# A streaming-encoder block on eight cores: first-pass gates block by block with weight slots of their own, and both first FFN units in slices of K

## The chip, the cores and the metric

The kernel runs on all 8 NeuronCores of one Trainium2 chip; cores 0 to 3 are one die, 4 to 7 the other. The cores share nothing while they run: each does one eighth of the sequence positions, and loads all weights itself. The metric is the device time of the slowest core in microseconds. Everything below is read from one profiled execution, on its slowest core (core 7), unless another is named.

## The reference, cut to what matters

```python
def reference(x, c, ...):          # x (2, 8192, 1024); D_FF 2816, 8 heads of 64
    mod = silu(c) @ w_ada + b_ada  # shift, scale, gate for each of three sub-layers
    h = modulate(rms_norm(x, g_ffn1), sh1, sc1)
    a, b = split(h @ w_ffn1_in)
    x = x + 0.5 * gt1 * ((silu(a) * b) @ w_ffn1_out)

    h = modulate(rms_norm(x, g_mix), sh2, sc2)
    q, k, v, u, ga, gb = split(h @ w_in)
    ya = chunk_band_attention(q, k, v, ...) @ w_attn_out  # own chunk of 64 and 8 before it
    yb = multiscale_pool(u, w_pool_group, pool_scale) @ w_pool_out
    x = x + gt2 * ((sigmoid(ga) * ya + sigmoid(gb) * yb) @ w_o)

    h = modulate(rms_norm(x, g_ffn2), sh3, sc3)
    ...                                                   # a second FFN like the first
    return x
```

## The kernel before, in words

A core owns 2048 positions, held transposed (features on partitions) as four blocks of 512 columns, blocks 1 to 4, and recomputes one more block ahead of them, block 0 (the halo), because attention and pooling look back. Three stages follow each other: the first FFN over blocks 0 to 4, the mixer, and the second FFN over blocks 1 to 4. Nearly all TensorE work is matmuls of 128x128 weights against 512 columns in bf16, eight of them (over K) for one output tile.

**The order is planned, not written.** The code emits operations through `S.op` with an engine, a cost, what it reads and writes, and a priority (`S.prio`). `Sched.schedule` then simulates the five engines and picks, for each, the ready operation with the lowest priority number that can start first. The resulting list of each engine is fixed in the program; every engine then works through its list strictly in order. In the mixer the priorities come from the table `RAMPS`: for instance "a0" is the first attention pass, "k3" and "q4" are key and query projections, "g0" the gates of the first pass. The planner also simulates the DMA queues (`drain`), with a latency and a share for GpSimd's and SyncE's queue. A change of a number in the table, or of a rule in the planner, moves work on every engine.

**The start.** SyncE loads the halo and block 1; GpSimd loads the first eight chunks of `w_ada` (conversion from f32 to bf16 in the DMA) with the first FFN weight tile `W1ST` between chunks 5 and 6. Each `w_ada` chunk feeds 16 one-column matmuls (`ada_mm`, L573), whose result is a piece of shift or scale. Chunks 4 to 7 bring the scales: after each, `norm_late` (DVE L675, ACT L671) makes two of the eight 128-row slices of the normalised input of blocks 0 and 1. `norm_late(1, ...)` stands behind the loop over the chunks in the code. A `unit` is one hidden tile of the FFN for one block: eight matmuls for the a half, eight for the b half, then SiLU on ACT and a product on DVE. The very first unit (block 0) is issued slice by slice as the input slices appear (L729, 16 matmuls in all); every other unit is issued whole (L738). Block 2's x is loaded by SyncE once the last `w_ada` chunk (`ADA[7]`) is in.

**The mixer** works in two passes over the owned blocks, 1 and 2 and then 3 and 4. Queries, keys and values are projected (`kq_unit` L922 with a one-matmul sum of squares L929, `v_tile` L905); `att_pair` handles two heads and 256 queries: three groups of score matmuls (L968), exponentials on ACT, multiplication with a bias table on DVE, 20 matmuls with V (L1004), a normalisation and a transposition (L1017). `u_stage` is the pooling branch (L1048, L1062, L1087). `gates` computes, for each of eight output tiles n and each of the pass's two blocks mb, two 8-matmul gate tiles (L1116), two 4-matmul branch tiles (L1129), and their gated sum into `MRG`. `oproj` (L1148) multiplies `MRG` with `w_o`. PSUM has eight banks, and the planner places each tile.

**Weight places.** A load takes the next slot of a ring of 4 KB slots per partition. Ring "m" has six slots and serves queries, keys, values, gates and `w_o`. The gates of a pass use three tiles per pair of output tiles, twelve loads in all, each used for both blocks. Ring "u" is one slot, `o_wx`, in the x buffer of block 4, which is spilled to memory in the meantime. A load whose slot is still read waits on GpSimd's queue, and everything behind it in that queue waits too.

## Time and profile before

| | us |
|---|---|
| three runs | 1826.21, 1827.65, 1531.79 (median 1826.21) |
| the profiled execution, its own time | 1537.52 |
| its span, first to last instruction, core 7 | 1535.9 |
| spans of the eight cores | 1522.5 to 1535.9 |
| busy: TensorE | 1482.4 |
| busy: VectorE | 853.5 |
| busy: ScalarE | 471.4 |

The span is the time between the first and the last instruction of a core; the execution's own time is 1.6 us more. "Busy" of TensorE counts matmuls; weight loads overlap them. The granted clock is 1.00 at 2.4 GHz and 0.50 at 1.2 GHz. The three runs lie at two levels; the profiled execution is at the lower one. The first FFN runs until about 640 us, the mixer until about 1070, the second FFN from there to the end.

### The profile page before, as it was taken

To read this page: it belongs to the slowest core of one execution; us is meant where nothing else is said; L and a number is where in the kernel's file an instruction comes from. 1 tells how busy PE (TensorE), PEld (TensorE's weight loads), DVE (VectorE), ACT (ScalarE), POOL (GpSimd) and SP (SyncE) were. 2 spreads that over 40 slices of the span, in tenths; PEclk is the share of its full clock that TensorE was granted. 3 is DMA by queue.
4 is the path that set the end of the run, shared out by engine and by line. 5 is a ranking of instruction groups with operands and counts; after the bars stand their busy time and mean duration, and the time that the engine had idled before them with its cause. 6 is when DMAs were issued, how large, how long until landed. Compare 5 with 4: busy or idle time off the path is not lost.

```text
span 1535.9 us, 22662 instructions; the slowest of 8 cores (1522.5 to 1535.9 us)
## 1 busy us (share of the span) xinstructions
PE 1482.4 (97%) x7952; PEld 695.3 (45%) x7952; DVE 853.5 (56%) x1336; ACT 471.4 (31%) x658; POOL 104.7 (7%) x146
## 2 busy tenths in 40 slices
PE   2899999999999999999999999999999999999998
PEld 1344444444444444455554544444444444444443
DVE  2365557374484745677865668456352616262644
ACT  3460110101101046787775551345401010101010
POOL 1100000000000012200000000302000000000000
PEclk8799999999999999999999999999999999999999
DMA  9946443524415110420053355348033221211022
GB/s 207 246 84 103 87 133 77 152 61 123 135 39 143 22 44 1 142 52 15 2 124 56 58 101 104 55 83 135 10 56 56 42 41 22 42 28 28 1 110 110
DMA packets 28478, 120.21 MB, mean 78 GB/s; under 512 B 3280, under 2 KB 3536, under 8 KB 26320
## 3 DMA queue, kind: packets, MB, share of 16 engines
q0 software_dynamic: 17856, 63.09, 24.6%
q1 hardware_dynamic: 10512, 55.67, 10.4%
q8 instruction: 67, 1.10, 0.3%
q14 instruction: 43, 0.35, 0.1%
HBM read 169.24 MB, written 12.58 MB: 118 GB/s over the span
## 4 chain that ended last, share of the span: by engine, by line
PE 92%; DMA 3%; DVE 2%; ACT 1%; issue 1%; POOL 0%; DVEq 0%; ACTq 0%; POOLq 0%; SPq 0%
PE ps L738 44%; PE ps L771 22%; PE ps L1116 7%; PE ps L922 4%; PE ps L1129 4%; PE ps L1148 3%; PE ps L905 2%; DMA arena<-w_ada 2%; PE ps L1062 2%; PE ps L968 1%; PE ps L1004 1%; PE ps L630 1%; ACT arena L514 1%; DVE arena L520 1%; DMA arena<-w_adat 1%
## 5 line engine op out<-in xcount | busy, mean ns | idle before, releaser
L738 PE MATMUL ps<-arena 128*128 128x512 bf16 x3152 | 691.3, 381 | 2.8 <-DVE arena L520 2.7
L514 ACT ACTIVATE arena<-ps 128x512 bf16<-128x512 f32 (+3 forms) x426 | 269.7, 652 | 936.2 <-PE ps L738 770.1
L738 PEld LDWEIGHTS ps<-arena 128*128 128x128 bf16 x3152 | 309.3, 98 | 380.4 <-issue 19.1
L526 DVE SCALAR_TENSOR_TENSOR arena<-ps,arena 128x512 f32<-128x512 f32 (+1 forms) x500 | 359.8, 747 | 76.2 <-ACT arena L514 19.7
L771 PE MATMUL ps<-arena 128*128 128x512 bf16 x1584 | 348.2, 381 | 1.9 <-DVE arena L520 1.1
L520 DVE TENSOR_TENSOR arena<-arena,ps 128x512 bf16<-128x512 bf16 x198 | 135.1, 686 | 367.2 <-PE ps L738 357.1
L771 PEld LDWEIGHTS ps<-arena 128*128 128x128 bf16 x1584 | 155.5, 98 | 191.3 <-issue 11.6
L520 DVE TENSOR_TENSOR arena<-arena 128x1024 bf16<-128x1024 bf16 (+10 forms) x229 | 174.7, 779 | 44.5 <-ACT arena L514 38.1
L1116 PE MATMUL ps<-arena 128*128 128x512 bf16 x512 | 116.2, 379 | 0.6 <-DMA arena<-w_gate 0.6
L514 ACT ACTIVATE arena<-arena 128x512 f32<-128x512 f32 (+2 forms) x87 | 90.5, 1054 | 42.8 <-DVE arena L526 26.5
L604 DVE SCALAR_TENSOR_TENSOR arena<-arena 128x1024 f32<-128x1024 f32 x48 | 58.7, 1224 | 64.2 <-DMA arena<-w_adat 63.7
L1116 PEld LDWEIGHTS ps<-arena 128*128 128x128 bf16 x512 | 48.9, 98 | 59.2 <-issue 1.4
L526 DVE SCALAR_TENSOR_TENSOR arena<-arena,ps 128x512 f32<-128x512 f32 x64 | 43.8, 686 | 50.9 <-PE ps L1129 45.9
L922 PE MATMUL ps<-arena 128*128 128x512 bf16 x288 | 67.5, 382 | 0.2 <-ACT arena L515 0.2
L1129 PE MATMUL ps<-arena 128*128 128x512 bf16 x256 | 60.6, 379 | 0.4 <-DVE arena L526 0.4
L1148 PE MATMUL ps<-arena 128*128 128x512 bf16 x256 | 59.2, 387 | 0.5 <-ACT arena L514 0.5
L515 ACT ACTIVATE arena<-arena 128x512 bf16<-128x512 f32 x63 | 48.2, 805 | 18.0 <-DVE arena L520 18.0
L520 POOL TENSOR_TENSOR arena<-arena 128x1024 bf16<-128x1024 bf16 x18 | 38.5, 2144 | 114.0 <-ACT arena L514 114.0
L922 PEld LDWEIGHTS ps<-arena 128*128 128x128 bf16 x288 | 27.5, 98 | 32.0 <-issue 3.5
L1148 PEld LDWEIGHTS ps<-arena 128*128 128x128 bf16 x256 | 25.2, 99 | 31.4 <-issue 5.7
L515 ACT ACTIVATE arena<-ps,arena 128x512 f32<-128x512 f32 x50 | 34.2, 684 | 14.2 <-PE ps L630 6.9
L905 PE MATMUL ps<-arena 128*128 128x256 bf16 x320 | 37.8, 273 | 0.3 <-ACT arena L515 0.3
(67 smaller groups left out, 489.7 us busy)
## 6 DMA issues: line engine op xcount, KB each, us to landing
arena<-w_adat SPq DMA_DIRECT2D x48, 512.0 KB, 4.1
arena<-w_gate POOLq DMA_DIRECT2D x24, 512.0 KB, 7.3
arena<-w1i POOLq DMA_DIRECT2D x22, 512.0 KB, 8.2
arena<-w3i POOLq DMA_DIRECT2D x22, 512.0 KB, 5.2
arena<-x SPq DMA_DIRECT2D x5, 2048.0 KB, 14.8
outT<-arena SPq DMA_DIRECT2D x7, 1024.0 KB, 3.9
arena<-w_ada POOLq DMA_DIRECT2D x12, 512.0 KB, 24.3
arena<-w1o POOLq DMA_DIRECT2D x10, 512.0 KB, 8.1
```

The source lines that it names most:

```text
L514: return e.activation(out=o, in_=i, func=func, scale=scale)
L515: return e.activation(out=o, in_=i, func=func, bias=bias, scale=scale)
L520: return e.tensor_tensor(out=out() if callable(out) else out, in0=in0() if callable(in0) else in0, in1=in1() if callable(in1) else in1, op=op)
L526: return e.scalar_tensor_tensor(out=out, in0=in0() if callable(in0) else in0, scalar=scalar, in1=in1() if callable(in1) else in1, op0=op0, ...
L604: S.op("dve", lambda e: e.scalar_tensor_tensor(out=wt, in0=wt, scalar=1.0, in1=CCB, op0=ALU.mult, op1=ALU.mult, accum_out=MOD[:, j:j + 1]) ...
L738: ins = e.matmul(pst(t), lhsT=w[:, kt, :], rhs=hk(b, kt), start=(kt == 0), stop=(kt == 7))
L771: ins = e.matmul(pst(t), lhsT=wos[jl // 2][:, c0:c0 + 128], rhs=hd[jl], start=(jl == 0), stop=(jl == nk - 1))
L905: ins = e.matmul(pst(tl, hf * 256, hf * 256 + 256), lhsT=H[:, b, kt, t * 128:(t + 1) * 128], rhs=w[:, kt, :], start=(kt == 0), stop=(kt == 7))
L922: ins = e.matmul(pst(raw), lhsT=w[:, kt, f * 128:(f + 1) * 128], rhs=hk(b, kt), start=(kt == 0), stop=(kt == 7))
L1116: ins = e.matmul(pst(tg), lhsT=wg[:, kt, fs], rhs=hk(b, kt), start=(kt == 0), stop=(kt == 7))
L1129: ins = e.matmul(pst(ty), lhsT=w[:, hp, fs], rhs=src[:, hp, ms], start=(hp == 0), stop=(hp == 3))
L1148: ins = e.matmul(pst(to), lhsT=w[:, kt, (n % 2) * 128:(n % 2 + 1) * 128], rhs=MRG[:, kt, ms], start=(kt == 0), stop=(kt == 7))
```

## The change

1. `RAMPS` is a new table of numbers, with an entry "g0a" for the gates of block 1 alone. The planner's DMA model is changed: a landing latency `DLAT` of 2.6 instead of 2.0, and a transfer doesn't move before this latency has passed.
2. `gates(0, ...)` is split. The gates of block 1 are emitted right behind the pooling stage, with a ring "e" of three slots: two in the second half of `MRG`, and `o_wx`. The gates of block 2 stand where both stood, with ring "m". All twelve weight tiles are loaded once for each block, so the first pass has 24 gate loads. `MRG` is laid out by block, so that block 1's half is whole while the other half holds weights.
3. The first unit of block 0 and the first unit of block 1 are issued together in pieces of two K slices (`pieces`, L732): for each pair of slices, block 0's a and b, then block 1's a and b.
4. `norm_late(1, ...)` moves into the loop over chunks; block 2's x is loaded behind `ADA[6]`; in block 2's first normalisation ACT does four slices of eight instead of three.

```diff
+    DLAT = 2.6
...
-                            work[k].pop(0)[1].fin = now + 2.0
+                        work[k].pop(0)[1].fin = now + self.DLAT
...
-    MRG = view(o_mrg, BF16, (8, 1024))
+    MRG = view(o_mrg, BF16, (2, 8, TB))
...
+             "e": [o_mrg + 8192, o_mrg + 12288, o_wx]}
...
-                if kt in ((1, 4, 7) if sub == 0 else (0, 1, 3, 4, 6, 7)):
+                if kt in ((1, 3, 5, 7) if sub == 0 and b == 2 else (1, 4, 7) if sub == 0 else (0, 1, 3, 4, 6, 7)):
...
-    norm_late(1, range(8))
+            norm_late(1, (2 * k, 2 * k + 1))
...
+        def pieces(wt, bs):
+            wv = [wt[:, 1024 * i:1024 * i + 1024].rearrange("p (k n) -> p k n", k=8) for i in range(2)]
+            tl = {b: (Tile(), Tile()) for b in bs}
+            for k in range(4):
+                for b in bs:
+                    for t, w in zip(tl[b], wv):
+                        def mm(e, t=t, w=w, b=b, k=k):
+                            ins = None
+                            for kt in (2 * k, 2 * k + 1):
+                                ins = e.matmul(pst(t), lhsT=w[:, kt, :], rhs=hk(b, kt), start=(kt == 0), stop=(kt == 7))
+                            return ins
+                        S.op("pe", mm, reads=[wt, H[:, b, 2 * k:2 * k + 2, :]] + ([t] if k else []), writes=[t],
+                             cost=mmc(2, 512), also=[tl[b][1]] if t is tl[b][0] and k == 0 else (), stream="ab")
+            return tl
+
+        def unit(jl, b, wt, last=False, pre=None):
...
-            split = first and ucount[0] == 0
+            split = pre is not None
+            if split:
+                ta, tb = pre
...
-                    for b, after in ((2, ADA[7][1]), (3, wl[2][1]), (4, wl[3][1])):
+                    for b, after in ((2, ADA[6][1]), (3, wl[2][1]), (4, wl[3][1])):
...
+                            pcs = pieces(wts[0], (0, 1))
                             for jl in range(nk):
-                                unit(jl, 0, wts[jl])
-                                unit(jl, 1, wts[jl])
+                                unit(jl, 0, wts[jl], pre=pcs[0] if jl == 0 else None)
+                                unit(jl, 1, wts[jl], pre=pcs[1] if jl == 0 else None)
...
-    def gates(pas, pr):
+    def gates(pas, pr, mbs=(0, 1), ring="m"):
...
-            wga_ = load("m", gate_d[3 * c])[0]
-            wgb_ = load("m", gate_d[3 * c + 1])[0]
-            wap = load("m", gate_d[3 * c + 2])[0]
+            wga_ = load(ring, gate_d[3 * c])[0]
+            wgb_ = load(ring, gate_d[3 * c + 1])[0]
+            wap = load(ring, gate_d[3 * c + 2])[0]
...
-                for mb in range(2):
+                for mb in mbs:
...
     u_stage(0, ramp(*R["u0"], 8))
+    gates(0, ramp(*R["g0a"], 8), (0,), "e")
...
-    gates(0, ramp(*R["g0"], 16))
+    gates(0, ramp(*R["g0"], 8), (1,))
```

Of the table, the line with "a0" before and now, and the new entry "g0a":

```diff
-         "a0": (5.02, 11.48), "u0": (10.18, 20.6), "k3": (13.33, 13.57), "k4": (11.61, 26.2),
...
+RAMPS = {"g0a": (9.83, 12.94), "nb": (-2.29, 8.29), "f2": (-9.48, -7.81), "f3": (3.97, 5.97),
...
+         "v0b": (16.07, 20.14), "a0": (2.73, 9.57), "u0": (11.7, 21.52), "k3": (15.22, 22.54),
```

**Where instructions move.** Names are line numbers of each version; equal neighbours are counted together.

TensorE at the start, before: the sliced unit of block 0 (L729) between the one-column matmuls of the `w_ada` chunks (L573), then whole units (L738).

```order
L573 MATMUL ps<-arena 128x1 x48
L729 MATMUL ps<-arena 128x512 x8
L573 MATMUL ps<-arena 128x1 x16
L729 MATMUL ps<-arena 128x512 x4
L573 MATMUL ps<-arena 128x1 x16
L729 MATMUL ps<-arena 128x512 x4
L738 MATMUL ps<-arena 128x512 x56
```

And now (L576 one-column matmuls, L732 sliced, L751 whole):

```order
L576 MATMUL ps<-arena 128x1 x64
L732 MATMUL ps<-arena 128x512 x16
L576 MATMUL ps<-arena 128x1 x16
L732 MATMUL ps<-arena 128x512 x6
L576 MATMUL ps<-arena 128x1 x16
L732 MATMUL ps<-arena 128x512 x10
L751 MATMUL ps<-arena 128x512 x40
```

Block 1's first 16 matmuls have moved from behind the last chunk to between the chunks: 16 stand ahead of chunk 6's matmuls instead of 8, 6 ahead of chunk 7's instead of 4, and 10 behind it instead of 4.

GpSimd's queue from the last fold of block 4 in the first FFN (TENSOR_TENSOR) to the first pass's gate weights, before:

```order
L520 TENSOR_TENSOR arena<-arena 128x1024
L868 DMA arena<-w_pg 128x512
L870 DMA arena<-ident 128x128
L498 DMA arena<-w_kqvu 128x2048 x2
L498 DMA arena<-w_gate 128x2048 x12
L498 DMA arena<-w_o 128x2048 x4
```

And now:

```order
L523 TENSOR_TENSOR arena<-arena 128x1024 x8
L501 DMA arena<-w_gate 128x2048 x2
L523 TENSOR_TENSOR arena<-arena 128x1024
L501 DMA arena<-w_kqvu 128x2048
L523 TENSOR_TENSOR arena<-arena 128x1024
L882 DMA arena<-w_pg 128x512
L501 DMA arena<-w_kqvu 128x2048
L884 DMA arena<-ident 128x128
L501 DMA arena<-w_kqvu 128x2048
L501 DMA arena<-w_gate 128x2048 x22
L501 DMA arena<-w_o 128x2048 x4
```

Two gate loads have moved ahead of the last folds, and 22 (with two ahead of them, 24) stand where 12 stood. Ten of the 22 are for ring "e", twelve for ring "m", mixed.

TensorE in the first attention pass, before: the end of the longest stretch that holds only attention (L968 scores, L1004 products with V, L1017 transpositions; the eight matmuls of 16 columns, L1048, are the pooling branch's halo), up to a key or query projection (L922). Its first three rows, L1017, L968 and L1004, stand just ahead.

```order
L968 MATMUL ps<-arena 128x128 x4
L968 MATMUL ps<-arena 128x256 x4
L1048 MATMUL ps<-arena 128x16 x8
L968 MATMUL ps<-arena 128x256 x4
L1017 MATMUL ps<-arena 128x128 x2
L968 MATMUL ps<-arena 128x128 x4
L968 MATMUL ps<-arena 128x256 x4
L1004 MATMUL ps<-arena 128x65 x20
L968 MATMUL ps<-arena 128x256 x4
L968 MATMUL ps<-arena 128x128 x4
L1017 MATMUL ps<-arena 128x128 x2
L922 MATMUL ps<-arena 128x512 x8
```

And now the longest such stretch (L982 scores, L1018 products, L1031 transpositions, L936 projection); one row of two score groups stands just ahead:

```order
L1018 MATMUL ps<-arena 128x65 x20
L982 MATMUL ps<-arena 128x128 x4
L982 MATMUL ps<-arena 128x256 x4
L1031 MATMUL ps<-arena 128x128 x2
L982 MATMUL ps<-arena 128x256 x4
L982 MATMUL ps<-arena 128x128 x4
L1018 MATMUL ps<-arena 128x65 x20
L982 MATMUL ps<-arena 128x256 x8
L1031 MATMUL ps<-arena 128x128 x2
L1018 MATMUL ps<-arena 128x65 x20
L982 MATMUL ps<-arena 128x128 x4
L936 MATMUL ps<-arena 128x512 x8
```

The stretch has moved to another place of the pass and holds three products with V instead of two.

## Rows read from the trace of the kernel before

**Rows 1.** The page, its first line and part 1: the span, and TensorE's busy time.

```profile
span 1535.9 us, 22662 instructions; the slowest of 8 cores (1522.5 to 1535.9 us)
...
PE 1482.4 (97%) x7952; PEld 695.3 (45%) x7952; DVE 853.5 (56%) x1336; ACT 471.4 (31%) x658; POOL 104.7 (7%) x146
```

**Rows 2.** Windows of 20 us: PE, PEld, DVE, ACT, POOL busy; clock, DMA share, GB/s.

```profile
40.00:60.00 20.00, 15.75 (x75) 6.48 (x76) 6.01 (x15) 5.90 (x9) 0.76 (x1) 0.59 1.03 224
120.00:140.00 20.00, 19.15 (x138) 9.22 (x137) 8.55 (x16) 2.61 (x4) 2.64 (x5) 0.91 0.71 130
```

**Rows 3.** Timeline of TensorE, 40 to 84 us: start, duration, line, count, idle before.

```profile
41.33 3.57 PE L729 MATMUL ps<-arena 128*128 128x512 bf16 x8 [3.23 <-DVE arena L675]
44.69 0.61 PE L573 MATMUL ps<-arena 128*128 128x1 bf16 x16
46.89 1.86 PE L729 MATMUL ps<-arena 128*128 128x512 bf16 x4 [1.59 <-ACT arena L671]
...
50.49 1.86 PE L729 MATMUL ps<-arena 128*128 128x512 bf16 x4 [1.33 <-DVE arena L675]
52.15 14.33 PE L738 MATMUL ps<-arena 128*128 128x512 bf16 x56
...
81.45 2.27 PE L630 MATMUL ps<-arena 128*128 128x512 bf16 x8
```

**Rows 4.** Windows of 4 us; the number after POOL is the granted clock.

```profile
52.00:56.00 4.00, 4.00 (x11) 1.33 (x10) 0.69 (x1) 2.01 (x3) 0.00 (x0) 0.50 0.99 270
56.00:60.00 4.00, 4.00 (x19) 1.79 (x18) 0.69 (x1) 0.79 (x2) 0.00 (x0) 0.96 0.99 282
```

**Rows 5.** Timeline of SyncE's queue, 40 to 84 us.

```profile
47.21 17.71 SPq L802 DMA_DIRECT2D arena<-x  x3
```

**Rows 6.** DMA queues, 36 to 44 us: queue, packets, MB, share of 16 engines.

```profile
q0 software_dynamic: 358, 1.32, 100.3%
```

**Rows 7.** DMA queues, 54 to 62 us: same columns.

```profile
q1 hardware_dynamic: 112, 1.57, 56.3%
q0 software_dynamic: 151, 0.55, 45.3%
```

**Rows 8.** Timeline of ScalarE, 75 to 90 us: block 2's last normalised slice.

```profile
81.92 0.80 ACT L515 ACTIVATE arena<-arena 128x512 bf16<-128x512 f32 x1
```

**Rows 9.** Windows of the mixer stage, same columns as rows 2.

```profile
640.00:980.00 340.00, 330.32 (x2538) 175.63 (x2537) 237.92 (x440) 204.15 (x302) 30.52 (x39) 1.00 0.33 68
680.00:760.00 80.00, 74.57 (x820) 45.49 (x818) 64.84 (x142) 62.37 (x89) 0.53 (x1) 1.00 0.05 8
900.00:920.00 20.00, 18.80 (x129) 8.96 (x128) 13.05 (x24) 9.71 (x14) 1.58 (x3) 1.00 0.63 116
```

**Rows 10.** Who TensorE waited for, 640 to 980 us: total us, times, longest.

```profile
PE ps L968 <- ACT arena L514: 3.3, 9, 0.6
```

**Rows 11.** Tile view of w_gate: issue to landing, all 24 loads.

```profile
DMA to landing us min/median/max: 5.1/7.3/9.0
```

**Rows 12.** Timeline of TensorE, 905 to 950 us: the one wait for a gate weight.

```profile
945.64 1.89 PE L1116 MATMUL ps<-arena 128*128 128x512 bf16 x8 [0.64 <-DMA arena<-w_gate]
```

**Rows 13.** Timeline of GpSimd, 938 to 948 us: the load behind that wait.

```profile
939.25 0.53 POOL L498 DMA_DIRECT2D arena<-w_gate  x1 [13.21 <-PE ps L1017]
```

**Rows 14.** Timeline of TensorE, 745 to 755 us: attention without other work.

```profile
748.29 0.39 PE L968 MATMUL ps<-arena 64*128 64x256 bf16 x4
748.62 0.78 PE L1004 MATMUL ps<-arena 128*128 128x65 bf16 x20
...
751.43 0.39 PE L968 MATMUL ps<-arena 64*128 64x256 bf16 x4 [0.54 <-ACT arena L514]
...
753.76 0.27 PE L1017 MATMUL ps<-arena 128*128 128x128 bf16 x2 [0.64 <-DVE arena L520]
```

**Rows 15.** Groups by line and form, 700 to 780 us: exponentials of scores, 512-column reads.

```profile
L514 ACT ACTIVATE arena<-ps 128x1024 bf16<-128x1024 f32 x26 | 25.7, 1023 | 4.2 <-PE ps L968 2.9 <-DVE arena L520 0.8 <-DVE arena L526 0.4
...
L514 ACT ACTIVATE arena<-ps 128x512 bf16<-128x512 f32 x28 | 16.4, 595 | 12.4 <-PE ps L922 9.6 <-DVE arena L1010 1.3 <-PE ps L968 1.3
```

More of the change, by code:

```diff
@@ L249, in drain @@
             while (work["pool"] or work["sp"]) and (until is None or now < until):
-                both = work["pool"] and work["sp"]
+                live = [k for k in work if work[k] and work[k][0][2] <= now + 1e-9]
+                both = len(live) == 2
                 share = {"pool": 1.0 - self.SPSHARE, "sp": self.SPSHARE} if both else {"pool": 1.0, "sp": 1.0}
-                step = min(work[k][0][0] / share[k] for k in work if work[k])
+                step = min([work[k][0][0] / share[k] for k in live] +
+                           [work[k][0][2] - now for k in work if work[k] and k not in live])
                 if until is not None:
@@ L255, in drain @@
                 now += step
[L256 to L260 removed]
+                for k in live:
+                    work[k][0][0] -= step * share[k]
+                    if work[k][0][0] <= 1e-9:
+                        work[k].pop(0)[1].fin = now + self.DLAT
             if until is not None:
@@ L1142, in oproj, with mmo @@
             to = Tile()
[L1144 removed]
+            def mmo(e, to=to, n=n, mb=mb):
                 ins = None
```

28 lines of the change are left out of this document (7 added, 21 removed), and 8 rows, old and new, of the table RAMPS.

## Prediction

> **What bounds the kernel now.** Look first at the page: TensorE is busy 1482.4 us of a span of 1535.9 [rows 1], so all its idle time together is 53.5 us. The change adds and removes no matmul (7952 before), so it can gain only idle time and time at the lower clock. Two per cent, which is about what a measurement of this kernel can tell from no change, are 30.7 us.
>
> Then the windows, to see where the idle time lies. The first sliced unit starts at 41.33 us [rows 3]; ahead of it stand loads whose order the change keeps. From 640 to 980 us, the mixer, TensorE is busy 330.32 of 340 us: 9.7 us idle. 5.4 of these lie between 680 and 760 us, in the first attention pass, and 1.2 between 900 and 920 [rows 9]. The FFN stages have almost none, and their order is nearly the same. So the change works on two places: the stretch from 41 to 84 us, and 9.7 us of the mixer.
>
> Last, the rows inside the two places. At the start the granted clock is 0.59 between 40 and 60 us [rows 2], 0.50 until 56 and 0.96 behind it [rows 4]: matmuls cost about double until then. In the mixer the waits are short and many: TensorE's scores (L968) waited for exponentials on ACT, 3.3 us in nine waits [rows 10].
>
> **The start, step by step.** Eight sliced matmuls take 3.57 us [rows 3], 0.446 each at 1.2 GHz; from 56 to 60 us, nearly all at 2.4 GHz, 4 us hold 19, 0.21 each [rows 4]. Before: 16 matmuls of block 0 are issued between the chunks, with idle gaps of 1.59 and 1.33 us for the slices, and block 1's 16 start at 52.15. Their end: 3.85 us at the low clock until 56.0 hold 8.6 matmuls, 7.4 more at 0.21 take 1.6, so 57.6 us.
>
> After, in the order shown: 16 matmuls from 41.33, at 0.446, end at 48.5. Chunk 6's one-column matmuls (0.61) were at 44.69 and now come behind them, a delay of 3.8 us for that chunk, and scale, slices and the rest are late with it: end 49.1. The gap of 1.59 stays, since the next six need that chunk: 50.7. Six matmuls: 53.4. Chunk 7: 54.0. Two matmuls hide 0.9 of the gap of 1.33: 55.3. The last eight: if the clock rises at 56 as before, 1.6 slow and 6.4 fast ones take 2.0, end 57.3. That is 0.3 us better than before. If the clock stays low to the end, 8 take 3.6: 58.9, so 1.3 worse. If the clock rises inside the first block of 16, say for its last four, then these and the 16 behind them cost 0.236 less each, 4.7 us in all: end about 54.2 at best, 3.4 better. I take 1.5 better, between the neutral case and the good one, because the change closes most pauses between 41 and 53 us, and the row before shows the clock coming back 4 us after TensorE had begun to issue without pause at 52.15. Ends: 1.3 worse, 3.4 better.
>
> The row shows what TensorE did: pauses of 1.33 to 3.23 us among short blocks, and a clock at 1.2 GHz until 56 [rows 3, 4]. The Trainium skill, "TensorE: Matmul & The Clock Gate", section "HAM oscillation — how this bites in real kernels", advises to run the K slices of a tile together ahead of a wait so that the array stays at full clock. By that rule 16 matmuls in a row ahead of chunk 6 would bring the good end and not the value taken; it has its place among the rivals.
>
> Is the gain kept? Block 2 must be normalised when blocks 0 and 1 are done. Its last slice was ready at 81.92 + 0.80 = 82.7 us, and TensorE began block 2 behind the eight sums, at 81.45 + 2.27 = 83.7 [rows 3, 8]: cover of 1.0 us. The change pays for this. Block 2's x was issued at 47.21 [rows 5] and is now issued behind chunk 6, whose matmuls ran at 44.69, so 2.5 us earlier or more, and one of VectorE's slices moves to ACT. So cover of 1.0 + 2.5 = 3.5 against a gain of at most 3.4. In return chunk 7 has a rival for bandwidth: alone GpSimd's queue moved 1.32 MB in 8 us, beside an x block 0.55 [rows 6, 7]. If the last 0.15 MB of chunk 7 go at 0.069 instead of 0.165 MB/us, it lands 1.3 us later, ahead of its place in TensorE's order (53.4, where it was 46.89 + 1.86 = 48.7): no cost. The next weight tiles come later too, by some 3 us, and are needed at 55 to 57; I leave 0 to 1 us for it and take 0. The move of `norm_late(1)` costs and brings nothing: VectorE's order at the start reads as before, since the planner had mixed the two already.
>
> **The mixer, step by step.** *Gate loads.* 12 more loads of 0.5 MB (f32 in memory) ride on queues whose DMA share is 0.05 between 680 and 760 us and 0.33 over the stage [rows 9]: bandwidth is no cost. What can cost is time to turn a slot round: the three slots of ring "e" hold just one group of weights, so each load waits for the last reader and must land before the group after it. Load issue to landing took 5.1 to 9.0 us, median 7.3 [rows 11]. In the new order I counted the TensorE work between release and next use for the ten loads concerned, at 1.7 us per eight matmuls and the attention times below: 9.0, 10.5, 10.5, 13.4, 9.0, 12, 14, 10, 10.3 and 12 us. Allowing 0.5 us until GpSimd issues, the median load has 1.2 us to spare in the tightest cases, the slowest is 0.5 late. The one measured case: a load issued at 939.25 with its use ready at 945.0 cost 0.64 us at 945.64 [rows 12, 13], with 6.4 us for it. So 0 for most; I take 0.5, ends 0 and 5 (ten times 0.5). That wait at 945.64 itself has 11 us of cover in the new order: gain 0.6. GpSimd's queue runs in order: behind the two early gate loads stand the last folds of block 4's sums; the slots are free once a bias table is exponentiated on ACT, and the square which the fold needs stands behind that on ACT anyway: 0.
>
> *Attention.* In the longest stretch without other work, TensorE spent 748.29 to 753.76 = 5.5 us, of which 0.54 + 0.64 = 1.2 idle [rows 14]. The new stretch has 6 large and 3 small score groups, 3 products with V (one is 0.78) and 2 transpositions: about 5.2 us of work when the older one's 4.3 is scaled up by one product and one score group less a transposition. ACT needs for its three pairs 3 x (2 x 1.023 + 0.595) = 7.9 us [rows 15]. So its idle time is between 1.2 (as measured) and 7.9 - 5.2 = 2.7 us; the old stretch is gone, -1.2. Net 0 to +1.5; take +0.5. For the remaining 4.2 us between 680 and 760 the ingredients are the same (k, q, v and pooling as filler), so what falls and what rises is open: -3 to +3, take -1. The gates of block 1, which ask most of TensorE and least of ACT, now fill the end of this pass and the begin of the next; but there (760 to 900) little idle time is left to take. *900 to 920 us.* 1.2 us idle there, where the last gate and first `w_o` matmuls met; their new places are apart: -0.6, ends 0 and -1.2.
>
> Sum of the mixer: 0.5 - 0.6 + 0.5 - 1 - 0.6 = -1.2. The layout of `MRG` changes no operand's contiguous 512 columns: 0.
>
> **The forecast.** -1.5 - 1.2 = -2.7 us on the profiled execution's own 1537.5, so 1534.8, or 0.2%. The runs shown lie at 1531.8 and at 1826 to 1828; the profile belongs to the lower, from which it is 5.7 off, and its median of 1826.21 says nothing on this execution. I give the time on the lower level, from its run: 1531.8 - 2.7 = 1529. At the upper level the same share would leave it unchanged within 4 us.
>
> **The rivals.** *The clock comes back inside the slices* (chance 0.15), as under the rule above: 3.4 at the start and 1.2 in the mixer, 1527. For it speaks the block of 16 matmuls without a pause, against it that TensorE pauses again behind it for 1.6 us. *The idle time of the mixer really closes* (0.20). For it: gates are large blocks of TensorE work with light ACT and DVE work, ready early. Most of 9.7 us goes, say 8, with 3 at the start: 1521. Against it: the attention pass already had filler at most places, and waited for ACT all the same.
>
> *Slower: ring "e" is turned too late* (0.12). Place: `gates` of block 1, four groups. If loads land 9 us or more behind their issue (two rings' loads are mixed in one queue, and six are at times issued together), each of three turns costs 2 to 3 us on TensorE, +8 us, with no gain in the start: 1539. It decides from a landing of 8.6 us in the tightest cases; against it stands the median of 7.3.
>
> *Slower: attention loses its filler* (0.15). The new stretch shows the upper bound and others join it: +2.7 + 3, start +1: 1537. By the Trainium skill, "TensorE: Matmul & The Clock Gate", section "A second HAM failure mode: psum-queue depth-cycling", frequent short pauses between groups of matmuls make the clock fall and rise again. As a mechanism here: more pauses in the first pass, and the clock at 0.5 for a while; one drop, as that between 120 and 140 us where 64 one-column matmuls ran and the mean clock was 0.91 [rows 2], costs 1.8 us, three 5.4: 1537 with the rest (0.03 of the 0.15). The trace disagrees with that rule so far: 5.4 us of pauses in 80, and clock 1.00 [rows 9].
>
> *It does not do what it says* (0.08): the slices give nothing and the orders are worth the same: 1531 to 1532.
>
> **How the numbers follow.** Forecast 0.30, the rivals as above. The bounds of the terms go from -3.4 - 8 to +1.3 + 8; the range 1519 to 1542 holds all but about one in six. A gain of 30.7 us would need more than all idle time outside the first 41 us; a loss of that size needs a queue held up for tens of us, which no bound shows. So faster 0.02, within 2% 0.95, slower 0.03.
>
> **What would show it.** In the new profile: the last of the 32 sliced matmuls ends between 54.2 and 58.9 us, with the granted clock of 44 to 56 us above 0.5 if the good end holds; TensorE doesn't wait before block 2's first unit; idle time of TensorE from 640 to 980 between 6 and 12 us; waits of L1130 or L1143 for w_gate below 1 us in total; the stretch of pure attention with 1 to 3 us idle. Wrong it would be if a wait for w_gate of over 2 us appears, if block 2's normalisation is waited for, or if idle time shows up in the FFN stages.

## The result and the profile after

The changed kernel takes 1535.6 us (median of nine runs, 1534.3 to 1538.6), the kernel before 1531.3 beside it. The ratio is 1.0029 with a 95% interval of 1.0020 to 1.0039: some 4.4 us slower, where I had forecast 2.7 us faster. Ratios, here and below, leave out executions in which one die ran at a lower clock than the other.

The profiled execution's page begins as follows [rows 1]. TensorE's busy time fell by 6 us at the same 7952 matmuls, since more of them met the full clock (mean of the first 84 us on core 7: 0.96 against 0.79). That is this core in these two executions and not the change: the median of the eight cores is 0.91 in both kernels. The span hardly moved, so idle time grew.

```profile
span 1535.2 us, 22697 instructions; the slowest of 8 cores (1526.1 to 1535.2 us)
...
PE 1476.4 (96%) x7952; PEld 693.6 (45%) x7952; DVE 853.2 (56%) x1335; ACT 482.0 (31%) x667; POOL 112.1 (7%) x158
```

The start on core 7, TensorE's timeline [rows 3]. The first block of 16 ran as counted, then 6, 2 and 8; the last sliced matmul ends at 54.48 + 3.57 = 58.05. Block 2's norm is waited for 0.33 us (at 80.90).

```profile
41.83 6.56 PE L732 MATMUL ps<-arena 128*128 128x512 bf16 x16 [3.26 <-DMA arena<-w1i]
...
50.48 2.00 PE L732 MATMUL ps<-arena 128*128 128x512 bf16 x6 [1.71 <-DVE arena L678]
...
52.75 1.01 PE L732 MATMUL ps<-arena 128*128 128x512 bf16 x2
54.48 3.57 PE L732 MATMUL ps<-arena 128*128 128x512 bf16 x8 [0.71 <-ACT arena L674]
...
80.90 3.40 PE L751 MATMUL ps<-arena 128*128 128x512 bf16 x15 [0.33 <-ACT arena L518]
```

The mixer's windows on core 7, columns as in [rows 9]:

```profile
640.00:980.00 340.00, 322.96 (x2483) 170.03 (x2482) 231.62 (x435) 217.02 (x312) 30.64 (x45) 0.99 0.49 84
640.00:660.00 20.00, 15.50 (x99) 9.47 (x98) 13.16 (x17) 14.31 (x22) 1.63 (x3) 0.97 1.00 213
660.00:680.00 20.00, 19.51 (x101) 9.37 (x99) 8.03 (x17) 14.44 (x22) 0.00 (x0) 0.94 0.11 28
680.00:700.00 20.00, 16.32 (x149) 8.89 (x149) 13.56 (x29) 15.69 (x24) 0.53 (x1) 0.91 0.21 27
680.00:760.00 80.00, 70.04 (x720) 42.46 (x721) 59.88 (x128) 54.72 (x80) 0.53 (x1) 0.98 0.06 8
900.00:920.00 20.00, 19.38 (x171) 9.76 (x170) 15.58 (x32) 13.63 (x20) 1.58 (x3) 1.00 0.83 165
```

Idle time of the stage went from 9.7 to 17.0 us, and from 660 to 700 us the granted clock is 0.94 and 0.91 where before had 1.00. The window of 640 to 660 us stands out: 4.5 us idle, and the DMA engines full. Before, the same window reads:

```profile
640.00:660.00 20.00, 19.75 (x118) 11.49 (x117) 15.74 (x18) 15.87 (x24) 5.79 (x5) 0.95 0.61 174
```

The wait behind it is found in three steps. TensorE's timeline of the changed kernel has one long wait, for ScalarE:

```profile
653.85 1.89 PE L1130 MATMUL ps<-arena 128*128 128x512 bf16 x8
658.49 3.29 PE L936 MATMUL ps<-arena 128*128 128x512 bf16 x8 [2.75 <-ACT arena L518]
```

ScalarE's timeline at that time: it had no work that it was allowed to begin, since the next in its list was the exponential of the bias table's second quarter (`tab`: four loads by SyncE, two exponentials of 128x640 for each), and that was still on its way.

```profile
651.85 0.63 ACT L517 ACTIVATE arena<-arena 128x512 f32<-128x512 f32 x1
656.30 1.36 ACT L517 ACTIVATE arena<-arena 128x640 bf16<-128x640 f32 x2 [3.82 <-DMA arena<-tab]
```

The tile view of `tab`, changed kernel first and then before: the slowest of four loads took 14.0 us from issue to landing, where it was 5.7.

```profile
DMA to landing us min/median/max: 4.6/5.8/14.0
```

```profile
DMA to landing us min/median/max: 3.7/3.8/5.7
```

What moves beside it: SyncE spills blocks 3 and 4 (2 MB each, issued at 625.92 and some 8 us later) and GpSimd has the first two gate loads of ring "e" in flight from 630.56 on. Cores 0, 6 and 7 show 3.7, 4.5 and 4.5 us of idle time from 640 to 660; they have the longest spans (1532.9, 1534.9, 1535.2). Core 2 with 0.6 us there has the shortest, 1526.1, and a clock of 1.00 from 640 to 760 us.

Who TensorE waited for from 640 to 740 us on core 7, first the changed kernel, then before:

```profile
PE ps L982 <- ACT arena L517: 3.2, 7, 0.8
PE ps L936 <- ACT arena L518: 2.8, 1, 2.8
PE ps L943 <- ACT arena L517: 1.4, 4, 0.6
PE ps L1031 <- DVE arena L523: 0.9, 2, 0.5
PE ps L919 <- ACT arena L518: 1.1, 1, 1.1
PE ps L1062 <- DVE arena L535: 1.1, 1, 1.1
PE ps L1018 <- DVE arena L1083: 0.9, 1, 0.9
PE ps L1101 <- ACT arena L518: 0.7, 1, 0.7
PE ps L936 <- DVE arena L535: 0.5, 1, 0.5
PE ps L1076 <- DVE arena L535: 0.5, 1, 0.5
```

```profile
PE ps L968 <- ACT arena L514: 2.3, 6, 0.6
PE ps L1004 <- ACT arena L514: 0.7, 1, 0.7
PE ps L929 <- ACT arena L514: 0.7, 3, 0.2
PE ps L1017 <- DVE arena L520: 0.3, 1, 0.3
```

Attention (L982, L1018, L1031; before L968, L1004, L1017) waited 3.3 us before and 5.5 now. Projections (L919, L936, L943; before L922, L929) and pooling (L1062, L1076, L1101) waited 0.9 us before and 8.7 now, shorter rows of 0.2 to 0.4 us included in all four sums. So most of the loss isn't in the attention, but in the work meant to fill it; 2.8 us of it are the one wait behind the late table. For `w_gate` seven cores never wait, the eighth 0.3 us.

### The profile page after: what moved, and what is told of

Read it like the earlier page. It is cut to its first block, busy times and chain, and to the rows that moved or that the text cites. A ratio compares the mean times of both kernels' runs of the same rounds, so it can differ in the third digit from the quotient of the medians.

```text
span 1535.2 us, 22697 instructions; the slowest of 8 cores (1526.1 to 1535.2 us)
## 1 busy us (share of the span) xinstructions
PE 1476.4 (96%) x7952; PEld 693.6 (45%) x7952; DVE 853.2 (56%) x1335; ACT 482.0 (31%) x667; POOL 112.1 (7%) x158
## 4 chain that ended last, share of the span: by engine, by line
PE 91%; DMA 3%; DVE 2%; ACT 2%; issue 1%; POOL 0%; DVEq 0%; ACTq 0%; SPq 0%; POOLq 0%
PE ps L751 43%; PE ps L784 21%; PE ps L1130 7%; PE ps L936 4%; PE ps L1162 4%; PE ps L1143 4%; DMA arena<-w1i 2%; PE ps L1076 2%; PE ps L919 2%; PE ps L982 1%; PE ps L1018 1%; DMA arena<-tab 1%; DVE arena L523 1%; ACT arena L517 1%; PE ps L732 1%
## 5 line engine op out<-in xcount | busy, mean ns | idle before, releaser
L751 PE MATMUL ps<-arena 128*128 128x512 bf16 x3136 | 681.5, 379 | 0.3 <-ACT arena L518 0.3
L751 PEld LDWEIGHTS ps<-arena 128*128 128x128 bf16 x3136 | 306.9, 98 | 370.9 <-issue 1.5
L784 PEld LDWEIGHTS ps<-arena 128*128 128x128 bf16 x1584 | 154.8, 98 | 188.9 <-issue 4.5
L523 DVE TENSOR_TENSOR arena<-arena 128x1024 bf16<-128x1024 bf16 (+11 forms) x229 | 174.7, 782 | 33.9 <-ACT arena L517 28.2
L1130 PEld LDWEIGHTS ps<-arena 128*128 128x128 bf16 x512 | 49.3, 98 | 59.0 <-issue 1.0
L936 PE MATMUL ps<-arena 128*128 128x512 bf16 x288 | 68.8, 385 | 3.6 <-ACT arena L518 3.1
L936 PEld LDWEIGHTS ps<-arena 128*128 128x128 bf16 x288 | 27.3, 98 | 36.0 <-issue 7.5
L919 PE MATMUL ps<-arena 128*128 128x256 bf16 x320 | 37.5, 273 | 1.8 <-ACT arena L518 1.1
```

What stands on the lines that cost most here:

```text
L523: return e.tensor_tensor(out=out() if callable(out) else out, in0=in0() if callable(in0) else in0, in1=in1() if callable(in1) else in1, op=op)
L751: ins = e.matmul(pst(t), lhsT=w[:, kt, :], rhs=hk(b, kt), start=(kt == 0), stop=(kt == 7))
L784: ins = e.matmul(pst(t), lhsT=wos[jl // 2][:, c0:c0 + 128], rhs=hd[jl], start=(jl == 0), stop=(jl == nk - 1))
L919: ins = e.matmul(pst(tl, hf * 256, hf * 256 + 256), lhsT=H[:, b, kt, t * 128:(t + 1) * 128], rhs=w[:, kt, :], start=(kt == 0), stop=(kt == 7))
L936: ins = e.matmul(pst(raw), lhsT=w[:, kt, f * 128:(f + 1) * 128], rhs=hk(b, kt), start=(kt == 0), stop=(kt == 7))
L1130: ins = e.matmul(pst(tg), lhsT=wg[:, kt, fs], rhs=hk(b, kt), start=(kt == 0), stop=(kt == 7))
```

## Experiments

Eleven kernels ran, ratios to the kernel before, five rounds each. With them the change comes apart into a front (start and first FFN) and a mixer.

### The start alone, in the old company

```diff
-    norm_late(1, range(8))
+            norm_late(1, (2 * k, 2 * k + 1))
...
-                    for b, after in ((2, ADA[7][1]), (3, wl[2][1]), (4, wl[3][1])):
+                    for b, after in ((2, ADA[6][1]), (3, wl[2][1]), (4, wl[3][1])):
...
+                            pcs = pieces(wts[0], (0, 1))
```

With `pieces` and the slices on ACT as in the change; nothing else of it.

> The kernel before, with only the start of the change: the two first units in K slices issued together, norm_late(1) in the loop, block 2's x behind ADA[6], four slices of block 2's norm on ACT. Table of numbers, planner's model, gates and rings are as before, so the mixer's order stays. My step for the start said 1.5 us faster (ends 1.3 slower, 3.4 faster). The trace after showed TensorE's idle time from 41 to 84 us about as before (3.9 against 4.4 us, median of cores). Theory A (the start is neutral, the loss is all in the mixer): 1530 to 1533, ratio to before 0.9995 to 1.0010. Rival (the start itself costs what the whole change lost): 1535 to 1536, ratio 1.0025 to 1.0035. My forecast's own step: 1529 to 1530, ratio 0.9985 to 0.9993.

Measured: 1531.6 us, 1.0007 (0.9998 to 1.0016). No gain. The timeline of core 4, whose clock was 1.00 from 48 to 64 us, shows one reason: the slices end early, and then TensorE stands at block 2's sums (and behind this wait, from 64 to 68 us, the clock is 0.57). The squares for them, on ScalarE, waited for block 2's x.

```profile
51.84 1.89 PE L729 MATMUL ps<-arena 128*128 128x512 bf16 x8 [1.59 <-ACT arena L671]
53.57 7.07 PE L748 MATMUL ps<-arena 128*128 128x512 bf16 x32
63.99 3.36 PE L630 MATMUL ps<-arena 128*128 128x512 bf16 x8 [3.36 <-ACT arena L514]
```

```profile
59.66 3.71 ACT L514 ACTIVATE arena<-arena 128x2048 bf16<-128x2048 f32 x2 [4.76 <-DMA arena<-x]
```

Cores 1, 4 and 6, with a mean clock of 0.93 to 1.00 from 41 to 60 us, wait 1.9 to 3.4 us between 60 and 84. The other five, with 0.59 to 0.78, are later and don't wait there. So the gain is eaten by this wait where the clock was high; elsewhere the low clock left none (before, the median clock of this stretch was 0.80, here 0.69). In the changed kernel the sums stand behind 40 matmuls of whole units instead of 32, and there is no such wait: the planner's longer landing time moved them.

### The changed kernel with the old start

```diff
-            norm_late(1, (2 * k, 2 * k + 1))
+    norm_late(1, range(8))
...
-                            pcs = pieces(wts[0], (0, 1))
```

The same hunks taken out of the changed kernel.

> The changed kernel with the start of before (one sliced unit, norm_late(1) behind the loop, block 2's x behind ADA[7], three slices on ACT); the new table, the planner's model and the split gates stay. Theory A (start neutral): like the changed kernel, 1535 to 1536.5, ratio to before 1.0022 to 1.0035. Rival (the start costs): 1531 to 1532. If the start gained 1.5 as forecast: 1537, ratio 1.004.

Measured: 1539.7 us, 1.0059 (1.0045 to 1.0074). Theory A (neutral start) fell, and so did both others of the expectation: in this company the start is worth 0.0030, 4.6 us, more than I had thought in any case.

### The front alone: changed front, old mixer

```diff
-                        work[k].pop(0)[1].fin = now + self.DLAT
+                        x = work[k].pop(0)[1]
+                        x.fin = now + (self.DLAT if x.idx < self.NEWTO else 2.0)
...
     ffn(w1i, w1o, 0, [0, 1, 2, 3, 4], True)
+    S.NEWTO = len(S.ops)
```

From operation `NEWTO` on the planner uses the old DMA model; `RAMPS`, gates, `MRG` and rings are as before, the start as changed.

> The start of the change and its planner's DMA model up to the end of the first FFN (a transfer lands 2.6 us after its end, and moves only 2.6 us after its issue); from the mixer on the planner counts as before, with the old table of numbers and unsplit gates, so the mixer's order is that of before. Theory E (the front part of the change is a gain, the mixer alone loses): TensorE's idle time from 140 to 560 us is 0 where it was 2.7 (median of cores), no wait of 3.4 us for block 2's sums at 64 us as in the run with the start alone, so 2 to 4 us better than before: 1526.5 to 1528.5, ratio 0.9974 to 0.9987. Rival (the front part gives back what it gains, as the run with the start alone did): 1530 to 1532, ratio 0.9995 to 1.001. My forecast's step for the start alone: 1.5 better.

Measured: 1527.5 us, 0.9980 (0.9971 to 0.9990): the front is a gain of 3.1 us, and this kernel beats both. Windows of core 7, this kernel and then before:

```profile
140.00:560.00 420.00, 420.00 (x1947) 190.38 (x1946) 251.14 (x378) 54.72 (x85) 17.96 (x28) 1.00 0.39 94
640.00:740.00 100.00, 94.92 (x872) 57.73 (x870) 76.45 (x152) 78.10 (x117) 2.36 (x4) 1.00 0.17 38
740.00:980.00 240.00, 234.46 (x1660) 116.60 (x1657) 156.30 (x284) 122.90 (x183) 23.68 (x32) 1.00 0.42 80
```

```profile
140.00:560.00 420.00, 417.21 (x1928) 188.20 (x1926) 251.64 (x379) 48.61 (x77) 16.29 (x28) 1.00 0.39 95
640.00:740.00 100.00, 95.55 (x808) 56.28 (x808) 76.55 (x144) 77.74 (x116) 6.85 (x7) 0.99 0.21 53
740.00:980.00 240.00, 234.77 (x1732) 119.35 (x1732) 161.37 (x297) 126.41 (x187) 23.68 (x32) 1.00 0.38 75
```

2.8 us idle in the first FFN are gone: four waits of up to 0.9 us of L738 for VectorE. The mixer isn't the same order (872 matmuls between 640 and 740 us instead of 808), but idles about as much as before, at a clock of 1.00.

### The planner's model in the front, with the old start

```diff
-            norm_late(1, (2 * k, 2 * k + 1))
+    norm_late(1, range(8))
...
-                            pcs = pieces(wts[0], (0, 1))
```

On the kernel above.

> As the kernel with the changed front and the old mixer, but with the start of before too: only the planner's DMA model in the first FFN is changed. Theory E: the waits of 2.7 us between 140 and 560 us go; but the changed kernel with the old start had 2.1 us of waits between 60 and 84 us for block 2's norm, where before had 0.3, so the two cancel: 1529.5 to 1531.5, ratio 0.9995 to 1.0005, and this kernel is 2 to 4 us slower than the one with the new start. Rival (the planner's model is the whole gain, and the start gives nothing in either company): 1528 to 1529, same as with the new start.

Measured: 1532.0 us, 1.0008 (0.9999 to 1.0018). A little above the 1529.5 to 1531.5 expected. So the front is two halves that only pay together:

| | old planner model | new model in the first FFN |
|---|---|---|
| old start | 1 | 1.0008 |
| new start | 1.0007 | 0.9980 |

With the old start and the new model TensorE waits 2.1 us (median of cores, 60 to 84 us) for block 2's sums and norm, which eats what the FFN gains; the new start brings block 2's x earlier (issued at 44.8 us instead of 46.7 on core 3) and takes this wait to 0.2. That is 1.9 of the 4.3 us between the two kernels. The clock from 41 to 60 us may hold the rest: its median over cores is 0.69 here and 0.91 with the new start, in one profiled execution of each.

### The gate loads held back

```diff
+            dp = [TABOP[1]] if ring == "e" and c == 0 else ()
-            wga_ = load(ring, gate_d[3 * c])[0]
+            wga_ = load(ring, gate_d[3 * c], deps=dp)[0]
```

The same for `wgb_`; `TABOP[1]` is the load of the bias table's second quarter.

> The changed kernel, but the first two gate loads of ring e wait until the bias table's second quarter (the one behind the spill of block 4 in SyncE's queue) has landed; after them the order of GpSimd's queue and a little of TensorE's moves. Theory B (the early gate loads share the DMA engines with the spills and with that table load, which landed 14.0 us after its issue on core 7 against 3.8 before, and ScalarE waited 3.82 us for it, TensorE 2.75 behind): the table lands within 6 us of its issue, ScalarE waits below 1 us for it on every core, TensorE's idle time from 640 to 660 falls from 3.1 us (median of cores) to about 1, time 1532.5 to 1534. Rival C (the spill ahead of it on SyncE's queue makes it late, not the gate loads): it still lands 10 us and more behind its issue, time as changed, 1535 to 1536. Rival D (the wait is covered or replaced: what is lost is in the new order of 660 to 740 us): the landing improves and the time stays at 1535 to 1536.

Measured: 1549.5 us, 1.0128 (1.0113 to 1.0142). No theory held. From 640 to 660 us idle time fell from 2.8 to 0.8 us (median of cores), and the slowest table load on core 7 took 8.6 us instead of 14.0. But theory B wanted 6 us and no wait of 1 us on any core: on cores 0, 2, 4 and 5 it took 10.9 to 11.7 us, and ScalarE waited 2.0 to 2.8. And the planner answered the late weights with another order, with 3.8 us idle from 660 to 680 (changed: 2.3) and 7.7 us from 860 to 980 (changed: 1.4). The time says nothing on the table.

### The exponentials moved on ScalarE

```diff
     S.schedule()
+    qa = S.q["act"]
+    for r, behind in ((2, 9), (3, 9), (6, 8), (7, 8)):
+        i = qa.index(TEXP[r])
+        qa.insert(i + behind, qa.pop(i))
```

> The changed kernel with all DMA as it is, but on ScalarE the four exponentials of the bias table's second and fourth quarter stand nine and eight places further back in the engine's list (about 6 us later), behind key projections' LN and EXP chains; nothing else moves. Theory B2 (the in-order stall of ScalarE is what the late table costs): the wait for tab falls from 3.82 us on core 7 to below 0.5, TensorE's idle 640 to 660 from 3.7, 4.5 and 4.5 us on cores 0, 6 and 7 to 1 to 2, and the slowest cores gain 2 to 3 us: 1532.5 to 1534. Rival D (another wait takes its place within 20 us, since these cores' ScalarE is as late with its work as before): 1535 to 1536, with the idle time moved to 660 to 700.

Measured: 1532.4 us, 1.0013 (1.0004 to 1.0022). Moving four instructions of 0.7 us by some 6 us gives back 0.0016 of 0.0029, 2.5 us. Core 7:

```profile
640.00:660.00 20.00, 19.39 (x123) 11.68 (x122) 12.43 (x16) 15.30 (x25) 1.63 (x3) 1.00 0.80 153
660.00:680.00 20.00, 17.48 (x95) 7.58 (x95) 10.32 (x23) 16.07 (x26) 0.24 (x1) 1.00 0.12 34
680.00:700.00 20.00, 16.81 (x171) 9.65 (x169) 16.14 (x35) 14.63 (x21) 0.29 (x1) 1.00 0.15 28
640.00:740.00 100.00, 89.21 (x783) 49.84 (x781) 68.67 (x140) 76.64 (x115) 2.15 (x4) 1.00 0.22 44
```

The table load is as late as without the edit (13.1 us from issue on core 7), and nobody waits for it. From 640 to 740 us 10.8 us of pauses remain (median of cores; changed: 12.6). So theory B2 holds: the late table had cost the wait. Whether it had also cost the clock isn't shown. In this profiled execution the granted clock is 1.00 from 640 to 700 us on all cores, but two kernels below, without the wait too, have it down to 0.91 from 680 us on. Over the timed runs the mean clock of all cores is 0.993 both here and in the changed kernel.

### The table ahead of the second spill

```diff
     S.schedule()
+    qs = S.q["sp"]
+    i = qs.index(TABOP[1])
+    qs.insert(i - 1, qs.pop(i))
```

> The changed kernel, and on SyncE's queue the second quarter of the bias table is issued ahead of block 4's spill, where it stood behind it; nothing else moves in any engine's list. The table waits for block 3's spill to land, so block 4's spill is issued when that is done. Theory B (spills, early gate loads and the table share the DMA engines between 626 and 656 us, and ScalarE stalls in order): without the second spill beside it block 3's spill and the table land early, by 648; ScalarE doesn't wait for tab; TensorE's idle 640 to 660 is about 1 us, and the granted clock stays at 1.00 from 640 to 720: time as with the moved exponentials, 1531.5 to 1533, ratio 1.001 to 1.002. Rival (the early gate loads alone delay it by 8 us): the table lands at 652 or later, ScalarE still waits over 1 us, time 1534 to 1536.

Measured: 1534.2 us, 1.0021 (1.0011 to 1.0032). On core 7 the slowest table load takes 5.9 us, idle time from 640 to 660 is 1.1 us (median of cores). That is the mechanism by a second way, and it shows what makes the table late: early gate loads, but the second spill issued behind the table load: 5.5 to 6.8 us on the eight cores; both spills ahead of it, but no early gate loads (the kernel without the split, below): 6.2 to 7.3; both, as in the changed kernel: 11.3 to 14.0. The time decides nothing: 1534.2 lies just inside the rival's 1534 to 1536, the ratio just above theory B's 1.001 to 1.002, and the interval overlaps that of the moved exponentials. Over its timed runs the median span of all cores is 1527.1 us as with the moved exponentials (1527.0), while that of the slowest core is 1532.4 against 1530.3. In the profiled execution, the fastest of all at 1529.1, three cores show a clock of 0.90 to 0.93 from 680 to 740 us. Why the slowest core loses 2 us stays open.

### An exponential for the tanh

```diff
-                        act(sg, lambda tg=tg: pst(tg), AF.Tanh, scale=0.5, reads=[tg], writes=[sg], cost=0.6, tset=TANH)
+                        act(sg, lambda tg=tg: pst(tg), AF.Exp, scale=0.5, reads=[tg], writes=[sg], cost=0.6, tset=TANH)
```

On the kernel with moved exponentials; it no longer computes the sigmoid of the gates.

> The kernel with the moved bias-table exponentials (1532.4, ratio 1.0013), with an exponential in place of the tanh of all gates: the same tiles and instruction, a wrong function. The exponential needs no other ACT table than LN and EXP beside it; the changed kernel loads tables 12 times from 640 to 980 us on core 3, 1.28 us each, where before loaded one. Theory F (the table loads at 675 to 680 make pooling and TensorE late, 2.5 us idle from 660 to 680 where before has 0.5): 1530 to 1531.5, ratio 0.9998 to 1.0007, idle time 660 to 680 below 1.5. Rival (table loads are covered, ScalarE has 6 us and more of idle time in each 20): 1532 to 1533.

Measured: 1531.9 us, 1.0004 (0.9995 to 1.0013). ScalarE's groups from 640 to 980 us on core 7 show what it removes, first the changed kernel, then before:

```profile
L517 ACT ACT_TABLE_LOAD x7 | 9.0, 1283 | 0.1
...
L518 ACT ACT_TABLE_LOAD x6 | 7.7, 1283 | 1.1 <-PE ps L943 1.0
```

```profile
L514 ACT ACT_TABLE_LOAD x1 | 1.3, 1283 | 0.0
```

Thirteen loads of 1.28 us where there was one, since tanh now stands among LN and EXP; without it there is none in this stretch. Idle time from 660 to 680 fell from 2.5 to 1.6 us, from 760 to 860 from 0.5 to 0 (medians of cores). The gain of 0.0009, 1.4 us, is within the two intervals, so at least most of the 17 us was covered. But the profiled execution has a lower clock than that of the moved exponentials, 0.95 to 0.98 from 640 to 740 us on all eight cores, although it idles less there (9.3 us, median of cores). Core 7:

```profile
700.00:720.00 20.00, 16.51 (x178) 8.98 (x177) 13.40 (x30) 15.62 (x23) 0.00 (x0) 0.86 0.00 1
```

### The new numbers without the split

```diff
-    gates(0, ramp(*R["g0a"], 8), (0,), "e")
...
-    gates(0, ramp(*R["g0"], 8), (1,))
+    gates(0, ramp(*R["g0"], 16))
```

With `gates`, `MRG` and the rings of before.

> The changed kernel without the split of the gates: new table of numbers, planner's model and start as changed, but gates of blocks 1 and 2 together behind the attention pass with ring m, twelve loads, and MRG as before. No tanh stands among the LN and EXP chains of the first pass, and no gate load beside the spills. Theory F (gates early in the first pass are what costs: two extra ACT table loads of 1.28 us at 675 to 680 and the late bias table): 1529 to 1532. Rival G (the new numbers alone make the first pass worse, with or without gates in it): 1534 to 1537. TensorE's idle time from 640 to 740 tells them apart: before 6.1 us by the medians of its windows, changed 13.7; F says below 8, G above 11.

Measured: 1541.0 us, 1.0068 (1.0055 to 1.0081). Theory F fell: the new order loses with no gate in the first pass, and no late table either (7.3 us at most, on core 1). That is rival G in kind, but neither number of it: the time is above its 1537, and the 9.1 us idle from 640 to 740 (median of cores; before 4.7) are below its 11; 6.3 us more lie between 740 and 860 (before 2.7). Again the clock is below 1:

```profile
660.00:680.00 20.00, 17.05 (x103) 7.43 (x102) 11.44 (x23) 17.14 (x27) 0.00 (x0) 0.87 0.00 1
```

What loses is the new table and the planner's new DMA model in the mixer together; no run separates the two. Given both, the split is a gain of 0.0039, 6 us: from 740 us on its gates fill what the attention leaves (8.7 us idle up to 980 without it, 2.6 with it, sums of medians).

### The split in the old order

```diff
+    HOLD.append(KQL[0])
-    gates(0, ramp(*R["g0"], 16))
+    gates(0, ramp(*R["g0a"], 8), (0,), "e")
+    gates(0, ramp(*R["g0"], 8), (1,))
```

On the kernel with the changed front and the old mixer; `KQL[0]` is the last operation of block 4's keys, for which the loads of ring "e" wait, and "g0a" is (12.9, 13.55) beside the old numbers.

> The fastest run so far (changed start and planner's model for the first FFN, old table of numbers: 1527.5, ratio 0.998) plus the split of the gates: MRG by block, ring e, weights loaded twice. The loads of ring e wait for block 4's keys, so no gate stands early; TensorE's order is that of the kernel without the split up to the first gate, and behind it block 1's gates come first, then block 2's. Theory H (the split itself is neutral; new numbers and early gates made the loss): ratio 0.997 to 0.999, 1526 to 1529. Rival I (the split costs by itself: ring e of three slots is turned between four groups of weights, and there is no attention work of ten us between them here): waits for w_gate above 4 us in total between 800 and 900 us, 1532 to 1536. Rival J (it gains, as block 1's output projection may begin early): 1524 to 1526.

Measured: 1537.2 us, 1.0039 (1.0025 to 1.0054), against 0.9980 without the split. TensorE's waits of core 7 from 760 to 860 us:

```profile
PE ps L1149 <- DMA arena<-w_gate: 2.0, 2, 1.7
PE ps L1136 <- DMA arena<-w_gate: 1.9, 2, 1.6
PE ps L1136 <- ACT arena L519: 1.6, 1, 1.6
```

Core 3 has no wait for `w_gate` and a span of 1524.6; core 7 has 3.9 us of them, ScalarE's 1.6, and 1535.6. Where gates follow gates, ring "e" is turned too late, and how much too late depends on the core: 0 us of such waits on cores 3 and 4, 0.5 to 2.6 on five others. So my rival is real, in a place the change itself avoids, but it is a part only: from 760 to 860 us core 7 idles 10.2 us instead of 1.3 without the split, and core 3 5.1, of which 3.0 are its attention's scores waiting for ScalarE and VectorE. Theories H and J fell.

### One number set back

```diff
-         "a0": (2.73, 9.57),
+         "a0": (5.02, 11.48),
```

(On the kernel with moved exponentials.)

> The changed kernel with moved bias-table exponentials (1532.4, ratio 1.0013), with one number pair of the table set back: "a0" (5.02, 11.48), as before, for (2.73, 9.57). The first attention pass is spread over more key, query and value work, and ends later. Theory K (the new a0 is early against its fillers, so that the pass runs dry at 690 to 725 us): idle time of TensorE 640 to 740 falls from 10.8 us (median of cores) to 7 or below, time 1528 to 1530. Rival L (no single number does it; fillers spent earlier are missing later, the pauses move): idle 640 to 760 stays at 10 to 13, time 1531 to 1535.

Measured: 1553.2 us, 1.0149 (1.0132 to 1.0165). Theory K fell, and rival L was right only that the pauses move: idle time from 640 to 740 is 8.7 us (median of cores), from 740 to 860 another 13.3, and neither foresaw a loss of 21 us. Core 7:

```profile
740.00:760.00 20.00, 16.02 (x168) 8.17 (x165) 12.92 (x29) 11.19 (x14) 0.53 (x1) 0.66 0.01 2
760.00:860.00 100.00, 92.27 (x741) 48.38 (x738) 63.77 (x123) 65.36 (x92) 5.99 (x12) 0.97 0.48 85
```

## Why the prediction was wrong

**The sum.** By the runs the front is -3.1 us (0.9980) and the mixer +7.5 (1.0029 against 0.9980), where I had -1.5 and -1.2. The sign went wrong in the mixer. Of its 7.5 us, 2.5 are shown to be the late table, by moving the exponentials; the other 5 belong to the new order, and they are placed by idle time and waits, not undone by a run. That 1535.6 still lies in my range is luck: its upper end had room for late gate weights and for the attention, and not for what filled it. And the measurement tells more than the 2% that I had named: its interval is some 0.1% to either side.

**The step that failed** is "*Attention.* ... For the remaining 4.2 us between 680 and 760 the ingredients are the same (k, q, v and pooling as filler), so what falls and what rises is open: -3 to +3, take -1", and, under it, the frame "the change works on ... 9.7 us of the mixer". That frame counts only idle time that is there. 640 to 680 us had 0.7 us of it on core 7 and so no term; it now has 5.0. From 680 to 760 idle time rose from 5.4 to 10.0. The fillers are the same, but each is a chain through ScalarE and VectorE (square, LN, EXP; window sums), and, as I read the waits, the new order asks for their results sooner: 7.8 us more waits in projections and pooling (2.8 of them the late table), 2.2 in attention (640 to 740 us). The experiment without the split shows that the new table and the planner's new model in the mixer do this without any early gate; which of the two, and which number, stays open.

**"Bandwidth is no cost"** failed too. I read the DMA share where the gates would run (0.05) and the stage's mean (0.33). The first two loads don't go there: they move at 630 to 650 us, beside two spills, where the share was 0.61 and became 1.00. The price wasn't a late gate weight but a late bias table, and ScalarE in order behind it: 2.5 us by the moved exponentials. I had even looked at what is queued behind these loads, but on GpSimd's queue, not at what shares the engines.

**What was never priced:** the ACT table loads, 12 more of 1.28 us. Some 1.4 us, within the noise.

**The start.** The mechanics came out as counted (16, 6, 2, 8; end at 58.05 within 54.2 to 58.9; clock from 52 to 56 us 0.50 on core 7, 1.00 on cores 1, 5 and 6, 0.73 to 0.84 on the rest). Its worth was mis-sized in both companies: +1.1 with the old planner's order (zero lies in its interval), -4.6 in the changed kernel, -4.3 in the front alone, against -1.5 with ends of +1.3 and -3.4. I had checked block 2's normalisation against the gain, but not the sums ahead of it, whose place the planner's model decides; and I had read "the FFN stages have almost none" past 2.8 us of waits between 140 and 560 us, which that model takes away.

**Gate weights.** Right for the change: 0.3 us of waits for `w_gate` on one core, none on seven, though landings on core 7 reached 19.6 us; the wait at 945 us is gone. The rival "ring e is turned too late" doesn't act here; in the split in the old order it does, for up to 3.9 us.

**The smaller terms.** 900 to 920 us: 1.2 to 0.6 idle, as taken. The pure attention stretch (722 to 729 us) has 3.0 us of pauses, where I allowed 2.7. From 740 to 980 idle time fell from 5.2 to 2.6: gates fill that part, as I had argued. Over the whole stage it is 17.0 us, where I had named 6 to 12 as the sign of being right.

**The rivals.** "Attention loses its filler" named the nearest time (1537), and its clock part, which I had given 0.03 and held to be refuted by the trace, took place: 0.91 to 0.94 over 40 us on core 7. Its reason was half right: fillers didn't run out, they weren't ready. The rule of the Trainium skill that I had set against the trace ("TensorE: Matmul & The Clock Gate", section "A second HAM failure mode: psum-queue depth-cycling", frequent short pauses make the clock fall) fits these rows better than I had thought: seven of eight cores of the changed kernel show 0.93 to 0.98 from 640 to 740 us. But how much pause lowers the clock can't be read from the runs: with 10.8 us of short pauses in these 100 it held on seven of eight cores (moved exponentials), with 9.3 of them it fell on all eight (no tanh).

## What to carry to other kernels

When an order changes, don't price only the idle time that is there: list the windows that are full today, and ask for each whether its work still comes behind what it waits for. A load that is issued early belongs to the window in which it moves; look at who else moves there, and at what stands in order behind the last of them. And test halves of a change together as well as alone: here two edits gained nothing each (1.0007 and 1.0008, both within noise of 1) and 0.0020 in common.

## What the runs showed of the hardware

A table load of 640 KB took 3.7 us at best on core 7 and 14.0 behind 4 MB of spills and three GpSimd loads of 512 KB.

The eight cores do the same work, but the kernels differ in how far they lie apart, and the time is that of the slowest. Over the changed kernel's nine runs the median span is 1524.4 for the fastest core, 1530.2 for all and 1534.0 for the slowest; before, in other runs, 1523.2, 1526.1 and 1528.8; with the moved exponentials 1524.4, 1527.0 and 1530.3. So the move of four instructions brought back most of the spread. Pauses in the middle don't make it by themselves: without the split, with 9.1 us of them and a clock below 1, fastest and slowest core are 6.0 us apart in the median run, before 6.4, in the changed kernel 9.1.

In the changed kernel cores with a mean clock lower by 0.01 are 5.6 us longer; before shows no such slope. The place of the low clock doesn't explain it: the front alone has a slope of 3.3 us with a clock of 1.00 from 640 to 740 us on all cores, while the changed kernel with the old start, whose clock there is 0.91 to 0.98, has 1.1. The slope goes with the new start under the planner's new model (2.8 to 5.6 us in all nine such kernels, 0 to 1.1 in the other four); why isn't shown.
